# A two-layer SSD and neighbourhood-attention backbone on one core: projections ahead of the turns at two stage starts, small loads in order of use, and value windows put together by DMA

## What is computed

```python
def _ssd_mixer(...):
    t = h @ w_in                                # z, x|B|C, dt of 2 x 32 heads
    xbc = jax.nn.silu(_dwconv(xbc_part, conv_w, conv_b))
    dt = jax.nn.softplus(dt + dt_bias);  A = -jnp.exp(a_log)
    a_cum = jnp.cumsum(dt * A, axis=2)          # chunked scan, forth and back
    ...
    return rms(y * silu(z)) @ w_out

def _na_mixer(...):
    q, k, v, g = h @ w_in                       # 16 heads of 64
    s_win = einsum(q, k[8 rows around]) * scale + bias   # 16 columns by a mask
    s = jnp.concatenate([s_win, q @ k_ctx * scale]);  p = jax.nn.softmax(s)
    o = einsum(p_win, v_win) + einsum(p_ctx, v_ctx)
    return (o * silu(g)) @ w_out
```

## Time and profile before

| | |
|---|---|
| runs of the kernel (3) | 2271.32 us median, 2268.11 to 2275.94 |
| the profiled execution | 2274.24 us; span 2272.4 us from first to last instruction |
| mean granted TensorE clock | 0.966 of full |
| busy in the span | TensorE 92%, weight loads 76%, VectorE 61%, ScalarE 50%, GpSimd 21% |
| DMA | 204.7 MB, mean 90 GB/s |
| stages, about | first to 95 us, SSD to 1200, middle to 1462, attention to the end |

### The profile page before, as it was taken

How to read it: one execution, slowest core, us unless ns; L and a number is a source line. 1 busy time by engine, 2 the same in 40 slices (tenths; PEclk the granted TensorE clock), 3 DMA queues, 4 the chain that set the end, 5 groups by cost and what they waited for, 6 DMA issues and landing times. The chain is left out here.

```text
span 2272.4 us, 35679 instructions
## 1 busy us (share of the span) xinstructions
PE 2086.1 (92%) x12490; PEld 1717.3 (76%) x12490; DVE 1396.0 (61%) x3285; ACT 1133.4 (50%) x2790; POOL 468.8 (21%) x452
## 2 busy tenths in 40 slices
PE   4699999999999999999976999699999999999797
PEld 2488888787878878787755888577877877877676
DVE  4475968879596887969584433414554554555652
ACT  4244747566573856657363332324544444444431
POOL 1012323233232323323220111310110110110300
PEclk9799999999999999999987999899999999999799
DMA  9512322222221212122127434221211211211433
GB/s 372 202 58 77 98 72 93 74 75 66 83 92 47 102 66 82 60 84 96 38 79 242 126 101 128 65 62 47 71 45 54 74 49 47 75 47 38 151 80 86
DMA packets 118685, 204.70 MB, mean 90 GB/s; under 512 B 29021, under 2 KB 79197, under 8 KB 116461
## 3 DMA queue, kind: packets, MB, share of 16 engines
q1 hardware_dynamic: 106988, 160.47, 22.4%
q10 hardware_dynamic: 11520, 41.95, 5.4%
HBM read 175.69 MB, written 28.65 MB: 90 GB/s over the span
## 5 line engine op out<-in xcount | busy, mean ns | idle before, releaser
L419 PE MATMUL sg_pP<-h_h_hi,h_whi 128*128 128x512 f32 (+1 forms) x1152 | 428.8, 372 | 0.0
L421 PE MATMUL sg_pP<-h_h_hi,h_wlo 128*128 128x512 f32 (+1 forms) x1152 | 410.1, 356 | 0.0
L420 PE MATMUL sg_pP<-h_h_lo,h_whi 128*128 128x512 f32 (+1 forms) x1152 | 409.0, 355 | 0.0
L419 PE MATMUL at_pP<-h_h_hi,at_whi 128*128 128x512 f32 (+1 forms) x640 | 254.4, 397 | 8.4 <-POOL at_wlo L2180 8.4
L421 PEld LDWEIGHTS sg_pP<-h_h_hi,h_wlo 128*128 128x128 f32 x1152 | 218.7, 190 | 31.5
L420 PEld LDWEIGHTS sg_pP<-h_h_lo,h_whi 128*128 128x128 f32 x1152 | 219.4, 190 | 29.6
L419 PEld LDWEIGHTS sg_pP<-h_h_hi,h_whi 128*128 128x128 f32 x1152 | 219.2, 190 | 29.2 <-issue 0.2
L421 PE MATMUL at_pP<-h_h_hi,at_wlo 128*128 128x512 f32 (+1 forms) x640 | 239.0, 374 | 0.0
L420 PE MATMUL at_pP<-h_h_lo,at_whi 128*128 128x512 f32 (+1 forms) x640 | 237.5, 371 | 0.0
L864 ACT ACTIVATE sg_S<-sg_rowb,sg_tab 128x128 f32<-128x128 f32 x640 | 195.9, 390 | 60.9 <-DVE sg_E L1126 56.1
L2180 POOL TENSOR_TENSOR at_wlo<-h_wr,at_whi 128x1024 fp32r<-128x1024 f32 x32 | 76.3, 2383 | 554.0 <-ACT at_whi L2050 554.0
(11 more groups left out here) (319 smaller groups left out, 4553.0 us busy)
## 6 DMA issues: line engine op xcount, KB each, us to landing
sg_rowb<-crows ACTq DMA_DIRECT2D x80, 512.0 KB, 3.7
h_wr<-in_w_ssd SPq DMA_DIRECT2D x48, 512.0 KB, 3.4
fs_w<-in_ada_w SPq DMA_DIRECT2D x16, 1024.0 KB, 8.8
h_wr<-in_w_na SPq DMA_DIRECT2D x32, 512.0 KB, 3.4
at_bias<-bt SPq DMA_DIRECT2D x256, 64.0 KB, 2.3
md_yr<-y SPq DMA_DIRECT2D x40, 256.0 KB, 3.3
fs_w<-in_ada_w SPq DMA_DIRECT2D x16, 512.0 KB, 8.3
y<-sg_Z SPq DMA_DIRECT2D x16, 512.0 KB, 3.0
```

What stands on the lines that cost most here:

```text
L419: pe.matmul(out, w_hi[:, k, :], h_hi[:, k, t0:t0 + n], start=(k == 0), stop=False)
L420: pe.matmul(out, w_hi[:, k, :], h_lo[:, k, t0:t0 + n], start=False, stop=False)
L421: x = pe.matmul(out, w_lo[:, k, :], h_hi[:, k, t0:t0 + n], start=False, stop=(k == KT - 1))
```

## The change

Three parts, in one diff.

In the SSD prologue the loads of `ident` and `bias` come first, with a semaphore `idl` of their own, then weight tile 1, then the other five on `small`. The turns of the time steps stand behind unit 0 and wait for `idl` alone; TensorE waits for `small` ahead of the cumulative sums, ScalarE ahead of the exponential of `alog`, VectorE ahead of scaling `par`.

In the middle stage the first attention weight tile is loaded and split while tile 9 is being multiplied, `x` of tile 9 is loaded into the free `yr`, and `turns(9)` stands behind the first two units of attention (v, blocks 0 and 1), which write the banks `pP`; attention starts with unit 2. `whi`, `wlo` and `pP` are allocated outside both stages; the six slots of `yhi` and `ylo` lie in `whi` and `wlo` and in a smaller own tile. Parts 0 to 5 of `h_hi` are written before the last products end (0 to 4 before), and their differences are shared out anew: VectorE 0, 1, 2, 5, GpSimd 3, 4.

In attention only the outer windows (columns 0 to 31 and 32 to 63) are copied from PSUM and turned, in three groups of 4, 4 and 2; `vt`'s two inner windows are put together by 16 DMAs a pair from the outer ones, inside SBUF. SP issues them ahead of the second weight tile of the next pair, and the first `values` of a pair waits for all.

```diff
@@ ssd_groups
+            sp.dma_start(ident[:, :], a["ident"]).then_inc(idl, 16)
+            sp.dma_start(bias[:, :], a["dt_bias"].partition_broadcast(P)).then_inc(idl, 16)
             load(1)
-            for dst, src in ((par, "conv"), (ident, "ident"), (le, "m_le"),
-                             (ge, "m_ge")):
-                sp.dma_start(dst[tuple(slice(None) for _ in dst.shape)], a[src]).then_inc(small, 16)
-
+            sp.dma_start(par[:, :, :, :], a["conv"]).then_inc(small, 16)
+            sp.dma_start(alog[:, :], a["a_log"].partition_broadcast(P)).then_inc(small, 16)
+            sp.dma_start(le[:, :], a["m_le"]).then_inc(small, 16)
+            sp.dma_start(ge[:, :], a["m_ge"]).then_inc(small, 16)
             sp.dma_start(dsk[:, :], a["dskip"].partition_broadcast(P)).then_inc(small, 16)
-            sp.dma_start(bias[:, :], a["dt_bias"].partition_broadcast(P)).then_inc(small, 16)
-            sp.dma_start(alog[:, :], a["a_log"].partition_broadcast(P)).then_inc(small, 16)
...
-            pe.wait_ge(small, 112)
-            for c in range(NCH):
...
             for q in range(PRO):
+                if q == 1:
+                    pe.wait_ge(idl, 32)
+                    for c in range(NCH):
...
+                    x.then_inc(ttr, 1)
                 if q == SUMS:
+                    pe.wait_ge(small, 80)
                     pe.wait_ge(tch, 16)
...
+            act.wait_ge(small, 80)
             act.activation(alog[:, :], alog[:, :], ACT.Exp).then_inc(tex, 1)
...
-            dve.wait_ge(small, 112)
+            dve.wait_ge(idl, 32)
             dve.wait_ge(ttr, 1)
...
+            dve.wait_ge(small, 80)
             chain(dve.tensor_scalar(par[:, :, :, :], par[:, :, :, :], 0.5, None, ALU.mult))
@@ middle
-        pa = [[m.ps(f"pa{i}{h}") for h in range(2)] for i in range(3)]
+        pa = [[m.ps(f"pa0{h}") for h in range(2)], pP, [m.ps(f"pa2{h}") for h in range(2)]]
...
-                if t + 1 < N:
+                if t + 2 < N:
                     sp.dma_start(x, x_in(t + 1)).then_inc(xl, 16)
-                else:
+                elif t + 2 == N:
+                    sp.wait_ge(yls, len(parts))
+                    sp.dma_start(turned(N - 1), x_in(N - 1)).then_inc(xl, 16)
                     sp.dma_start(xw[:, :, :], a["w_na"][0]).then_inc(first, 16)
...
+            pe.wait_ge(fwl, 1)
+            pe.wait_ge(sc, 2 * (N - 2))
+            for q in range(EARLY):
+                t0, n = BLOCKS[q]
+                pe.wait_ge(dlo, (2, 4)[q])
+                if q:
+                    pe.wait_ge(plo, 2)
+                project(pe, pP[q][:, 0:n], whi0[:, 0], wlo0[:, 0], h_hi, h_lo, t0, n)
             turns(N - 1)
...
                 if t == N - 2:
-                    for i in range(5):
+
+                    act.wait_ge(first, 16)
+                    act.wait_ge(yf, part_at[t, 3] + 1)
+                    act.activation(whi0[:, 0, :, :], xw[:, :, :], ACT.Copy).then_inc(fws, 1)
+                    for i in range(6):
                         part_hi(i)
...
                 if t == N - 1:
+                    pool.wait_ge(fws, 1)
+                    pool.tensor_tensor(wlo0[:, 0, :, :], xw[:, :, :], whi0[:, 0, :, :].bitcast(F32),
+                                       ALU.subtract).then_inc(fwl, 1)
                     part_lo(3)
                     part_lo(4)
@@ attention
-    VG = -(-(WIN + JC) // 4)
+    RG = GR // 4
+    SIDES = [0, CB - 1]
+    turned_at = [(0, 0, RG), (RG, SIDES[1] * RG, RG), (2 * RG, WIN, JC)]
+    VG = len(turned_at)
     VS = QT - VG
+    pieces = []
+    for cw in range(1, CB - 1):
+        for side in range(2):
+            lo, hi = max(K0C[cw], side * KC), min(K0C[cw] + KC, (side + 1) * KC)
+            pieces += [(cw, side, r * KC + lo - K0C[cw], r * KC + lo - side * KC, hi - lo) for r in range(4)]
...
+            def windows(p):
+                sp.wait_ge(vte, p * VG + 2)
+                for cw, side, dst, src, n in pieces:
+                    sp.dma_start(vt[dst:dst + n, p % 2, cw * RG:(cw + 1) * RG, :],
+                                 vt[src:src + n, p % 2, SIDES[side] * RG:(SIDES[side] + 1) * RG, :]).then_inc(vwin, 16)
...
                     if w:
-                        sp.wait_ge(wls, w)
+                        if w > 1:
+                            sp.wait_ge(wls, w - 1)
                         sp.dma_start(wr[:, :, :], a["w_na"][w]).then_inc(wld, 16)
                     w += 1
+                    if i == 0 and p:
+                        windows(p - 1)
...
             def values(n):
                 p, qt, rb, cb = rest(n)
+                if qt == 0:
+                    pe.wait_ge(vwin, 16 * len(pieces) * (p + 1))
...
-            for q in range(UPP):
+            for q in range(EARLY, UPP):
                 unit(q)
...
-                        for cw in range(CB):
-                            j = cw * (GR // 4) + (b - 1) * (QR // 4)
+                        for side in range(2):
+                            j = side * RG + (b - 1) * (QR // 4)
...
-            split(0)
             for q in range(UPP):
                 take(q)
```

More of the change, by code:

```diff
@@ L978, in _ @@
             pool.wait_ge(con, 5)
-            pool.wait_ge(small, 112)
+            pool.wait_ge(small, 80)
             def scaled(slot, g, c, lo):
@@ L1289, in _, with middle @@
                 norm_late(G - 1, c)
-def middle(nc, a, h_hi, h_lo, xw, y_dram, w_dram, scale, x_in, x_out, mod_rows, mod_cols, st_o, first, runs):
+def middle(nc, a, h_hi, h_lo, pre, pP, y_dram, w_dram, scale, x_in, x_out, mod_rows, mod_cols, st_o, runs):
+    xw, whi0, wlo0 = pre
     NH = D // 2
@@ L1668, in _ @@
                 if t == N - 2:
-                    for i in range(3):
+                    for i in (0, 1, 2, 5):
                         part_lo(i)
@@ L1700, in row_start, with attention @@
     return min(max(r - WR // 2, 0), GR - WR)
-def attention(nc, a, h_hi, h_lo, wr, first, bt_dram, y_dram, mod_rows, x_tile, out_tile, st_o):
+def attention(nc, a, h_hi, h_lo, pre, pP, bt_dram, y_dram, mod_rows, x_tile, out_tile, st_o):
     PR = NAH // 2
@@ L1984, in turn_values @@
                     pe.wait_ge(vte, v)
[L1985 to L1986 removed]
+                j, _, nv = turned_at[gidx]
+                for c in range(nv):
+                    x = pe.transpose(pT[:, c * P:(c + 1) * P], vv[:, j + c, :], ident[:, :])
                 x.then_inc(vtr, 1)
@@ L2042, in split @@
             def split(w):
-                if w:
-                    act.wait_ge(wld, 16 * w)
-                else:
-                    act.wait_ge(first, 16)
+                act.wait_ge(wld, 16 * w)
                 if w >= 2:
                     p, i = divmod(w - 2, len(KINDS))
-                    act.wait_ge(pj, done[p, KINDS[i]])
+                    act.wait_ge(pj, done[p, KINDS[i]] - EARLY)
                 act.activation(whi[:, w % 2, :, :], wr[:, :, :], ACT.Copy).then_inc(whs, 1)
@@ L2362, in program @@
         wr = m.sb("wr", [P, KT, P])
+        whi = m.sb("whi", [P, 2, KT, P], F32R)
+        wlo = m.sb("wlo", [P, 2, KT, P], F32R)
+        pre = (wr, whi, wlo)
         with ExitStack() as inner:
             mi = Mem(nc, inner, "h0")
-            whi = mi.sb("whi", [P, 2, KT, P], F32R)
-            wlo = mi.sb("wlo", [P, 2, KT, P], F32R)
             u = mi.sb("u", [P, UW])
-            pre = (wr, whi, wlo, u)
-            first_stage(nc, a, x0, h_hi, h_lo, pre, pad, mod_rows, mod_cols, kept)
-            ssd_groups(nc, a, h_hi, h_lo, pre, tabs, crows, pad, run, y0)
-        middle(nc, a, h_hi, h_lo, wr, y0, a["w_ssd_out"], a["norm_g"], x0, lambda t: rows(x1, t), mod_rows, mod_cols,
-               stored[0], first, (run, bt))
-        attention(nc, a, h_hi, h_lo, wr, first, bt, y1, mod_rows, lambda b, t: (b, patch(x1[CTX:TOK, :], t)),
+            first_stage(nc, a, x0, h_hi, h_lo, (wr, whi, wlo, u), pad, mod_rows, mod_cols, kept)
+            ssd_groups(nc, a, h_hi, h_lo, (wr, whi, wlo, u), tabs, crows, pad, run, y0)
+        pP = [m.ps(f"pP{i}") for i in range(2)]
+        middle(nc, a, h_hi, h_lo, pre, pP, y0, a["w_ssd_out"], a["norm_g"], x0, lambda t: rows(x1, t), mod_rows, mod_cols,
+               stored[0], (run, bt))
+        attention(nc, a, h_hi, h_lo, pre, pP, bt, y1, mod_rows, lambda b, t: (b, patch(x1[CTX:TOK, :], t)),
                   lambda b, t: (patch(out, t), b), stored[1])
```

79 lines of the change are left out of this document (41 added, 38 removed).

## The result

| | before | after |
|---|---|---|
| median of the runs (us) | 2270.53 (2268.11 to 2275.94) | 2244.02 (2241.19 to 2252.08) |
| ratio, 95% interval | | 0.988 (0.986 to 0.991) |
| span of the profiled execution | 2272.4 | 2250.3 |
| from the opening of the SSD stage to the end | 2176.7 | 2151.1 |

The change gained 26.5 us by the medians; 32 were forecast. The time, 2244.0, lies 4 us above the predicted 2240 and inside the range.

The account below looks back on a forecast made before the run. TensorE, busy 2086 of 2272 us, was taken as the bound. A 7.5, B 11.5 and C 13.0 sum to 32.0 us; from 2274.24 profiled that gives 2242.2, or 2239.3 as a median, stated as 2240, range 2232 to 2254.

Parts of the forecast that it names:

- A: SSD prologue: unit 0 starts without waiting for the small loads, TensorE 8.0 us earlier; gain 7.5 us, bounds 3.0 and 8.0.
- B: Passage from middle stage to attention: units 0 and 1 fill TensorE's wait; gain 11.5 us, bounds 6 and 13.
- rival 3: Middle stage: early units lack weights or parts and run behind the last turns; B loses 8.3, 2249 us; chance 0.06.
- its 0.7: Start of attention: weight load 2, behind 16 bias loads on SP's queue, has no slack; 0.7 us charged.
- A sign I had named for being wrong: Anywhere after the change: a new wait of ScalarE for weights above 3 us would show the forecast wrong.
- TensorE hardly pauses also keeps its clock: End of the middle stage: the last turns run at full clock, about 1.0 us instead of 1.97.
- C: Attention's value turns: three groups per head pair instead of five, plus window DMAs; gain 13.0 us, bounds 8.5 and 15.
- The steady gain: Seven pairs in attention: two fewer groups at 0.43 us each, 6.1, and six removed waits, 2.5.
- The clock: Start of attention's tiles: three groups instead of five avoid the half clock; gain 3.2 us, bounds 0 and 3.4.
- weight load 5: First attention tiles: this load stands behind the window DMAs on SP's queue; loss 1.5 us, bounds 0 and 4.
- rival 2: SP's queue at attention's start and tile 1: weight loads 2, 3, 5 late, 6 us in all, 2246; chance 0.13.
- Rival 4: Attention: the 16 window transfers follow one another, TensorE waits before value products; 2260 to 2371 us; chance 0.07.

Follow-up runs that it names:

- e1: The kernel before with only the SSD prologue change (small loads in order of use, unit 0 ahead of the turns): ratio 0.9967 to the kernel before, gain 8.2 us.
- e4: The changed kernel with a pair's window DMAs issued behind weight load (p, 1) instead of ahead: ratio 0.9852 to the kernel before, gain 34.5 us.
- e6: The changed kernel, tile 8 modulated before VectorE's fourth difference, squares' junk written over tile 9 of x (output wrong there): ratio 0.9879 to the kernel before.
- e2: The kernel before with only the middle-stage change (first attention weights early, units 0 and 1 there): ratio 0.9961 to the kernel before, gain 8.6 us.
- e5: The changed kernel run again without any edit: ratio 0.9900 to the kernel before, gain 22.5 us.
- e9: As e6 on the changed kernel, but the squares' junk goes to the buffer of the first attention weights: ratio 0.9871 to the kernel before, gain 30.5 us.
- e7: The changed kernel with the edits of e4 and e6 together: ratio 0.9844 to the kernel before, gain 35.8 us.
- e11: e10 with GpSimd's difference of part 7 moved behind its second power: ratio 0.9838 to the kernel before, gain 36.9 us.
- e10: The changed kernel with the edits of e4 and e9, and three output-weight loads ahead of the last bias loads: ratio 0.9827 to the kernel before, gain 41.7 us.

## Why the prediction was right, and where it was not

**A, right, its size known only roughly.** Forecast 7.5; 8.1 at unit 7 in after (7.8 to 9.1 in the ten traces with this part) and 9.3 at the end of the middle stage, 8.2 by e1's medians, whose interval is 4.6 to 10.5. The 8.0 earlier on TensorE came through whole; the 0.5 us charged for VectorE's and ScalarE's chain was not needed. Between unit 7 and the last products the traces differ with the same code (e1 gains 7.8 at the one and 5.0 at the other, e4 8.8 and 8.5, e6 9.1 and 11.1), so the 9.3 isn't a value of the part.

**B, the mechanism right, one step failed.** The early units ran where forecast (rival 3 is out), and weight load 2 delayed nothing: unit 3 waited 0.21 us for load 1 and no later unit waited for weights, so its 0.7 was not due. A sign I had named for being wrong did appear: ScalarE waited 4.97 us for load 1 and 5.75 for load 2, and TensorE paid only those 0.21. The step that failed is "TensorE hardly pauses also keeps its clock ... they take about 1.0". That rests on the chain of the last tile ending where it ended before. I had costed VectorE's longer list (four differences ahead of tile 8's modulation instead of three) and the new wait of the squares at nothing, without naming the work that hides them, and nothing does: the modulation stands behind the fourth difference, and the squares behind the modulation. It cost 0.9 us where GpSimd gave way (e2, e4) and 3.2 where VectorE did (after, e5); in the second case the pause was 4.4 instead of 2.1 us, the clock fell, and the turns lost 0.9 more. Without the charge of 0.7 the forecast is 12.2; less these 4.1, and less 0.8 in the new stage (unit 2 took 8.3 us instead of 7.7, and the wait of 0.21), it is 7.3, and 7.1 was measured. Unit 3 started 16.6 us earlier than before by the opening, not 19 to 20. e9 removed both orders, and the last turns stood 10.2 us behind the products again, as before.

**C, sizes off in both directions.** The steady gain was forecast at 8.6 and is 11.9. A group costs 0.59 us: I had compared a tile with a group with a neighbour without, and the neighbour had other work of its own; the same tile before and after (10.44 and 9.85) is the right pair, 14 times 8.3. The wait of the earlier trace rows gives 0.55 a pair instead of 0.41. Two groups in pair 0 gave 3.0 (2.7 forecast). The clock gave 2.3 (3.2 forecast), but the step behind it, that three groups instead of five keep the clock up, is not borne out: e1 kept it with five and e7 lost it with three. That the term came out was luck.

The term that was mis-sized most is weight load 5: 1.5 charged, up to 4 allowed, 6.6 lost, and 7.2 won back in e4. Two numbers made it. The window DMAs were priced by the bias loads, 0.5 us each, and take SP 0.755 each, 12.1 us instead of 8. And I let ScalarE's slack (5.46 us of idle time behind the split) absorb the lateness, although ScalarE's wish for it came forward by 18 us (from 1531.27 to 1513.1) and the second group, behind which the issues start, by only 13 (its successor's start, 1521.08 to 1508.07); the 5 between them are the two groups less and the faster tile 0. ScalarE wanted the weights at 1513.1 and got them 10.4 us later. This is rival 2's mechanism, for load 5 alone. The same queue, looked at once more, has the output weights behind the last windows: 1.4 us in the last pair that I had not looked for.

**Rival 4.** No value product waited for a window in any of the traces. In e4, where the windows of pair 0 go out behind load 5: first window issued at 1501.91, last issue ended at 1514.48, first value products of the pair at 1519.58 without a wait. The page "DMA: Bandwidth & Descriptors" of the Trainium skill gives a DMA a fixed cost of about 2.0 us, in its section on the path of DMAs that GpSimd issues; sixteen of them one behind another would be an estimated 32 us, and e4's values came 17.7 us behind the first issue. As the bias rows suggested, these costs overlap, and what adds up is the issue, 0.755 us each on SP.

In sum, 5.4 us more than forecast (A 1.8, the steady tiles 3.3, pair 0's groups 0.3) stand against 11.8 less (load 5 5.1, B 4.4, the tail 1.4, the clock 0.9): 32.0 became 25.6 by the traces, and it stayed inside the range partly because the errors had both signs.

## What to carry to other kernels

A transfer that is itself hidden still costs its issue time to everything behind it on its queue. List what stands behind it, with the time by which it is wanted after the change, not before; here one line moved won 7 us. An operation added to an engine's list ahead of a chain is never free because the engine is idle on average: name what in the chain stands behind it. And a step is best costed from the same step in two states, not from its neighbour.

## What the runs showed of the hardware

**VectorE and GpSimd held each other up for a whole instruction where both read the SBUF.** The sum of tile 9 takes 1.23 us alone (e11). Beside GpSimd's difference it ends 1.08 us after GpSimd does, wherever it began: in e10 at 1447.23 against 1446.15, in after at 1451.09 against 1450.01 (1448.13 + 2.96 and 1447.62 + 2.39). The scaling, with one input from SBUF, also waits for GpSimd's end: 2.84 us beside it (e11), 0.75 alone (e10). VectorE's product with a PSUM input does not: 0.74 us beside GpSimd's difference, as alone. These are the rows of after:

```profile
1447.36 0.74 DVE L1641 SCALAR_TENSOR_TENSOR md_o<-md_pa,md_rstd,md_G 128x512 f32<-128x512 f32 x1
1447.62 2.39 POOL L1593 TENSOR_TENSOR h_h_lo<-md_ht,h_h_hi 128x1024 fp32r<-128x1024 f32 x1 [0.97 <-ACT h_h_hi L1549]
1448.13 2.96 DVE L1645 TENSOR_TENSOR md_o<-md_o,md_yr 128x1024 f32<-128x1024 f32 x1
```

The one that comes second pays, and GpSimd's two differences take 5.74 or 6.76 us by who wins. The Trainium skill states this on the page "SBUF — State Buffer", section "SBUF: two separate sides": the two share a pair of ports, and a VectorE operation with two SBUF inputs or in a 2-port perf mode and a GpSimd operation take it as an exclusive lock for the whole instruction, whichever starts first. These rows, and those of the two starts in e4, agree with it. By the rule VectorE's four differences (1.21 us each alone) could have been given a bound for the wait behind GpSimd's two, which is the term that B lacked.

**SP's issue time depends on the transfer.** A copy from SBUF to SBUF of 24 or 8 partitions takes 0.72 to 0.79 us to issue, mean of 16, a bias load 0.46 to 0.58, a weight load mostly 0.35. Why, these runs don't show.

**The clock went with the wait at the last turns.** They ran at 1.00 behind a pause of 2.1 us or less (e2, e4, e9) and at 0.50 behind one of 4.4 us (after, e5) or 9.5 (before): 1.09 against 1.97 us for the same eight matmuls. At tile 0 no such reading holds: with TensorE busy for 15.20 of 18.00 us in both, the granted clock was 0.81 before and 1.00 in e1.
